# Branch gates of a transformer block through the hyperbolic tangent instead of the sigmoid

## The reference, cut to what matters

```
ya = einsum('bsw,wd->bsd', o_att, w_branch_att)
yh = einsum('bsw,wd->bsd', o_hg, w_branch_hg)
g = jax.nn.sigmoid(gate_logits.astype(f32)).reshape(B, S, N_BRANCHES, D)
merged = g[:, :, 0] * ya + g[:, :, 1] * yh
mixed = einsum('bsd,de->bse', merged, w_out)
x = x + gate1 * mixed
```

## Time and profile before

| | |
|---|---|
| median of 3 runs | 2164.25 us (2162.42 to 2166.67) |
| profiled execution, its own time | 2162.72 us |
| its span | 2160.9 us |
| TensorE matmul busy | 1957.4 us, 91% of the span |
| VectorE busy | 656.9 us, 30% |
| ScalarE busy | 450.5 us, 21% |
| mean granted TensorE clock | 0.964 |

### The profile page before, as it was taken

One profiled execution on the slowest core, in us unless ns is written; L12 is line 12 of the kernel. 1 busy time (PEld: TensorE's weight loads), 2 busy tenths in 40 slices (PEclk: granted clock), 3 DMA queues, 4 the chain that ended last, 5 costly groups with the idle time before them and its releaser, 6 DMA issues.

```text
span 2160.9 us, 20391 instructions
## 1 busy us (share of the span) xinstructions
PE 1957.4 (91%) x8746; PEld 1168.4 (54%) x8746; DVE 656.9 (30%) x915; ACT 450.5 (21%) x664; POOL 29.6 (1%) x41
## 2 busy tenths in 40 slices
PE   3989989899959999898989989898889999999998
PEld 2876766466833434343433434343334487888887
DVE  6474464472140020111002020111027713222333
ACT  4347455410010101010000101010020303222222
POOL 0000000000000000000000000000030000000000
PEclk9999999999979999999999999999989999999999
DMA  7211111475419999999999999999952013323210
GB/s 289 79 41 57 60 39 40 153 275 188 199 61 413 416 416 416 417 416 417 418 418 418 417 416 416 417 417 416 418 176 78 20 59 117 98 94 99 95 63 39
DMA packets 143791, 513.43 MB, mean 238 GB/s; under 512 B 7891, under 2 KB 70355, under 8 KB 107731
## 3 DMA queue, kind: packets, MB, share of 16 engines
q1 hardware_dynamic: 139328, 486.57, 57.3%
q10 hardware_dynamic: 4374, 25.56, 3.1%
HBM read 510.00 MB, written 2.10 MB: 237 GB/s over the span
## 4 chain that ended last, share of the span: by engine, by line
PE 69%; DMA 19%; DVE 5%; ACT 4%; issue 2%; SPq 1%; POOL 0%; ACTq 0%; DVEq 0%; POOLq 0%
PE ps L1015 12%; DMA work<-in_w_exp_up 10%; PE ps L492 6%; PE ps L979 6%; PE ps L515 5%; DMA ring<-in_w_exp_up 5%; PE ps L1158 5%; PE ps L1119 4%; PE ps L1118 4%; PE ps L1117 4%; PE ps L508 3%; PE ps L937 3%; PE ps L510 3%; PE ps L509 3%; PE ps L669 2%
## 5 line engine op out<-in xcount | busy, mean ns | idle before, releaser
L979 PE MATMUL ps<-work 128*64 128x512 f32 x1208 | 356.1, 594 | 28.4 <-DMA work<-in_w_exp_up 27.5
L979 PE MATMUL ps<-ring,work 128*64 128x512 f32 x720 | 219.4, 594 | 16.3 <-DMA ring<-in_w_exp_up 15.9
L979 PEld LDWEIGHTS ps<-work 128*64 128x64 f32 x1208 | 117.1, 137 | 204.2 <-issue 148.9
L1974 DVE TENSOR_TENSOR work<-work,ps 64x512 f32<-64x512 f32 x64 | 42.0, 691 | 486.9 <-ACT work L1490 486.3
L1490 ACT ACTIVATE work<-ps 64x512 f32<-64x512 f32 x64 | 32.6, 585 | 750.7 <-PE ps L979 750.7
L1015 PE MATMUL ps<-work 128*64 128x512 f32 x608 | 155.0, 661 | 4.7 <-issue 4.2
L492 PE MATMUL ps<-work,ring 128*128 128x512 f32 x320 | 139.1, 593 | 1.5 <-ACT work L1388 0.8
L1117 PE MATMUL ps<-xh,wh 128*128 128x512 f32 x352 | 137.0, 389 | 0.0
L1119 PE MATMUL ps<-xh,wl 128*128 128x512 f32 x352 | 136.9, 389 | 0.0
L1118 PE MATMUL ps<-xl,wh 128*128 128x512 f32 x352 | 136.9, 389 | 0.0
L979 PEld LDWEIGHTS ps<-ring,work 128*64 128x64 f32 x720 | 72.6, 137 | 119.0 <-issue 86.7
(11 more groups left out here) (253 smaller groups left out, 2444.4 us busy)
## 6 DMA issues: line engine op xcount, KB each, us to landing
work<-in_w_exp_gate SPq DMA_DIRECT2D x76, 1024.0 KB, 24.4
work<-in_w_exp_down SPq DMA_DIRECT2D x76, 1024.0 KB, 20.8
work<-in_w_exp_up SPq DMA_DIRECT2D x75, 1024.0 KB, 25.6
ring<-in_w_exp_gate SPq DMA_DIRECT2D x45, 1024.0 KB, 24.4
ring<-in_w_exp_up SPq DMA_DIRECT2D x45, 1024.0 KB, 25.5
ring<-in_w_exp_down SPq DMA_DIRECT2D x44, 1024.0 KB, 21.6
ring<-in_w_in SPq DMA_DIRECT2D x27, 1024.0 KB, 5.4
work<-in_ada_w ACTq DMA_DIRECT2D x16, 1024.0 KB, 5.1
```

The costliest lines, as they stand in the source:

```text
L979: i = e.matmul(PS[64 * gu:64 * gu + 64, fb, :], at(XET + 128 * k + 64 * z, 64), flat(key)[:, 512 * fb:512 * fb + 512], start=(k == 0), sto ...
```

## The change

All sixteen gate ACTIVATEs compute tanh of half the logit. The one that is missing is added by VectorE in the instruction that multiplies gate and branch product: a tensor_tensor becomes a scalar_tensor_tensor (in0 + 1.0) * in1. The factor one half is put on the copy of GATE1's row; GATE2's copy has the factor 1.0.

```
-                    e.activation(at(rooms(x), 512), bank(2), ACT.Sigmoid).then_inc(s["bg_a"], 1)
+                    e.activation(at(rooms(x), 512), bank(2), ACT.Tanh, scale=0.5).then_inc(s["bg_a"], 1)
...
-            def ada_row(n, dst):
+            def ada_row(n, dst, factor):
                 for i in range(2):
                     e.wait_ge(s["ar_pe"], n + i + 1)
-                    e.activation(at(dst + 512 * i, 512), bank(6 + i), ACT.Copy).then_inc(s["ar_a"], 1)
+                    e.activation(at(dst + 512 * i, 512), bank(6 + i), ACT.Copy, scale=factor).then_inc(s["ar_a"], 1)
...
-                e.activation(at(mt[4 * (d % 2)], 512), bank(4 * (d % 2)), ACT.Sigmoid).then_inc(s["mg_sa"], 1)
+                e.activation(at(mt[4 * (d % 2)], 512), bank(4 * (d % 2)), ACT.Tanh, scale=0.5).then_inc(s["mg_sa"], 1)
...
-                e.activation(at(mt[4 * (d % 2) + 1], 512), bank(4 * (d % 2) + 1), ACT.Sigmoid).then_inc(s["mg_sb"], 1)
+                e.activation(at(mt[4 * (d % 2) + 1], 512), bank(4 * (d % 2) + 1), ACT.Tanh, scale=0.5).then_inc(s["mg_sb"], 1)
...
-                    ada_row(0, GATE1)
+                    ada_row(0, GATE1, 0.5)
...
-            ada_row(2, GATE2)
+            ada_row(2, GATE2, 1.0)
...
-                e.tensor_tensor(at(s0, 512), at(s0, 512), bank(4 * (d % 2) + 2), ALU.mult).then_inc(s["mg_a"], 1)
+                e.scalar_tensor_tensor(out=at(s0, 512), in0=at(s0, 512), scalar=1.0, in1=bank(4 * (d % 2) + 2), op0=ALU.add, op1=ALU.mult).then_inc(s["mg_a"], 1)
...
-                e.tensor_tensor(at(s1, 512), at(s1, 512), bank(4 * (d % 2) + 3), ALU.mult).then_inc(s["mg_b"], 1)
+                e.scalar_tensor_tensor(out=at(s1, 512), in0=at(s1, 512), scalar=1.0, in1=bank(4 * (d % 2) + 3), op0=ALU.add, op1=ALU.mult).then_inc(s["mg_b"], 1)
```

## The result

The changed kernel runs in 2156.24 us (median of 5, 2154.68 to 2156.53) against 2164.25 before; the ratio is 0.9949 with an interval of 0.9938 to 0.9961. Two further comparisons gave 0.9949 (0.9928 to 0.9969) and 0.9950 (0.9938 to 0.9961). So it is 0.5% faster, about 11.0 us by the ratio, where 6.6 us were forecast. The two medians alone differ by 8.0 us, less than the ratio says, and 2156.24 lies inside the range; in the two further comparisons the medians differ by 11.5 and 12.3 us. The direction and the mechanism held, the size was too small.

What follows compares the result with a forecast made beforehand. TensorE bounds the kernel, so ScalarE's loads pay only where TensorE waits through them. Gains of 1.02 + 0.27 + 1.87 + 1.57 + 1.29 + 0.60 = 6.62 us, less 0.05, give 2157.7 us; range for 8 in 10: 2153.5 to 2163.

Steps and rivals of the forecast that it cites:

- The loads: ScalarE's table loads at the first eight gates, the attention's exponentials and the merge: 16 go, 20.5 us of ScalarE.
- the tables stay: Rival: Tanh has a load of its own and Exp is loaded back; about 2164.3 us, chance 0.10.
- The waits: TensorE's waits from 298.56 to 406.65 shorten by 1.02, 0.27, 1.87, 1.29 and 0.60 us without the loads.
- the two that were to stay: TensorE's waits of 2.67 us at 324.11 and 2.21 us at 373.65: nothing won at either.
- What is added: Tanh for Sigmoid taken as 0 us; VectorE's products with a scalar added taken as +0.05 us.
- The clock: TensorE's half clock behind the 3.03 us wait at 344.71 goes, worth 1.57 us.
- the fall at 324.11: Half clock behind TensorE's 2.67 us wait, L669 taking 3.65 us against 2.02: expected to stay, nothing won.
- this case for one place: The clock at 324.11 could hold by a small shift: 1.7 us more, a gain of 8.3 us.
- Slower by the clock: Rival: tables stay, waits grow and the clock falls at three more places; 5.2 us slower, 2169.4 us, chance 0.04.
- Given back behind the merge: Rival: TensorE waits for transfers behind the merge; gain only 0 to 4 us, 2160.3 to 2164.3, chance 0.07.

Runs made afterwards that it cites:

- before_again: The kernel before, without any edit, timed against itself: ratio 1.0009.
- merge_only_tanh: The changed kernel with the first eight gates sigmoids again (products times 2.0 for d < 4), tanh only in the merge: ratio 1.0004 to the kernel before.
- x0_sigmoid: The changed kernel with the gate x = 0 alone as a sigmoid, its product times 2.0: ratio 0.9981 to the kernel before.
- after_reorder: The changed kernel with the gate x = 2 and its rounding one step later on ScalarE and VectorE: ratio 0.9959 to the kernel before.
- reorder_dve: The changed kernel with the gate x = 2 one step later on ScalarE, VectorE's half subtraction two steps later: ratio 0.9935 to the kernel before.
- after_third: The changed kernel without any edit, compared a third time with the kernel before: ratio 0.9950.
- x3_sigmoid: The changed kernel with the gate x = 3 alone as a sigmoid, its product times 2.0: ratio 0.9981 to the kernel before.

## Why the prediction was right in kind and wrong in size

*The loads.* Right: 16 of 16 went, ScalarE's busy time fell from 450.5 to 429.9 us. The rival that the tables stay is out. What the trace of before couldn't show, a Tanh without a load behind Exp and in front of it, is there now, as the Trainium skill has it (ScalarE: Activation LUTs, "Table sets: the hidden batching unit"); its other rule, a logarithm and an exponential with one load, isn't what this program does in either trace.

*The waits.* Nearly right: 5.05 us forecast, 5.6 found (the stretch is 133.56 - 124.78 = 8.78 us shorter, and its two falls took 1.63 and 1.54). From mark to mark of TensorE: 1.1 for 1.02, 0.5 for 0.27, 2.0 for 1.87, 1.4 for 1.29, 0.6 for 0.60, and 0 for the two that were to stay. A load was priced 1.30 us, from its start to that of the next ACTIVATE. That was a little low: without a load the exponential starts before the rounding ahead of it has ended. Timelines of ScalarE, one line of the kernel before and two of the changed one:

```profile
293.62 1.05 ACT L1222 ACTIVATE fwh<-ring 128x1024 fp32r<-128x1024 f32 x1
```

```profile
294.00 1.05 ACT L1222 ACTIVATE fwh<-ring 128x1024 fp32r<-128x1024 f32 x1
...
294.94 0.68 ACT L1377 ACTIVATE work<-ps,stay 128x512 f32<-128x512 f32 x1
```

From the start of L1222 to that of the exponential it was 2.37 us and is 0.94, so a load on ScalarE's path is worth 1.43 us. No drain besides it showed.

*What is added.* Right: 0.60 us for Tanh; 0.68 to 0.69 for the product, so 0 where 0.05 was taken.

*The clock: the term that was mis-sized.* The forecast took back one fall, 1.57 us, and let the one behind the wait of 2.67 us "stay too". The price was right: traces show 1.54 us for the fall that was taken back. But the fall at 324.11, put at nothing, was worth 1.63, and the number of falls was taken as fixed: the first trace of before has two falls, two further traces of kernels with all eight sigmoids and their order unchanged have three, and none stands in the four traces of kernels with the first eight gates tanh and their order unchanged. So the clock had 3.2 us to give in the first trace and up to 1.6 more in the others, not 1.57. Together with the waits the stretch is 8.8 us shorter than in the first trace of before and 10.4 shorter than in before_again. The measured 11.0 us has an interval of about 2.5 to each side. The failing step was the inference from the lengths of the waits: that 2.67 us brings the clock down and 2.46, 2.21 and 2.12 don't. The same wait of 2.67 us came with a fall in four traces (before, before_again, merge_only_tanh, x0_sigmoid) and without one in six; 2.12 with a fall in two and without in two; 2.21 in after_reorder and reorder_dve with, in eleven without. The length is not nothing: 3.03 to 3.05 us had a fall in five of five, 2.46 in none of five. What decides besides the length seems to be where the wait lies in relation to what came before: x0_sigmoid left this wait its length and moved it by 1.1 us, and the fall came back. That rests on one trace of x0_sigmoid, and no run here shows how the chip chooses. The forecast had named this case for one place (8.3 us, with the clock at 324.11 holding; the traces have 8.8) and then gave it too little room; the case that the clock holds everywhere in the stretch should have been priced and the range have reached to 2152. That the result fell just outside the range and not just inside is chance: 0.3 us is far below what the runs can tell.

*Slower by the clock.* The rival was thought to need longer waits. after_reorder shows that a kernel with shorter waits can gain a fall: of 1.7 us won up to that fall, from the first wait on, the fall took 0.9 back.

*Given back behind the merge.* Half open. The profiled executions of before and after differ by 6.5 us only, because the part from the output projection on took 1635.44 in the one and 1637.76 in the other; but the changed kernel has 1635.16 in after_third, so that is no effect of the change. Between merge and output projection a wait for the branch weights of 2.2 to 2.6 us stands in three traces (before_again, x3_sigmoid, x0_sigmoid), with a fall beside it, and they take 117 us there where the others take 112.5 to 115. The same wait is 0.68 us in the first trace of before, 0.51 in that of the changed kernel and 1.80 in that of after_reorder. That would account for the ratios of x3_sigmoid and x0_sigmoid, and perhaps for a part of the 11.0 us. One trace for each kernel doesn't tell how often it comes, so it isn't shown.

## What to carry to other kernels

Price a table load only where the timeline has it between the engine's last input and the instruction that ends another engine's wait: of the 15 loads that went from this stretch about six moved the end at all, worth 5.6 of their 19.2 us. Then ask what the next engine in line allows; VectorE set the floor of two waits. And take the clock's falls in one trace as one draw: with waits of 2 to 3 us in a row, price every one of them with and without a fall, since a shift of 1 us far ahead of a wait may bring or take it.

## What the runs showed of the hardware that was not expected

The granted clock can fall to half behind a TensorE wait of 2.12 us (before_again) and hold behind one of 2.67 us (all four traces with the first eight gates tanh in their old order). The timing ahead seems to matter: with a wait 25 us earlier made 1.16 us longer, the clock fell behind an unchanged wait of 2.67 us, in the one trace of x0_sigmoid. Two traces of one program had two and three falls in the same stretch. A fall costs 1.3 to 1.6 us here with TensorE at work throughout, and 0.9 where a wait behind it took up part. A table load takes 1.28 us and moves the exponential behind it by 1.43: without it the exponential starts 0.11 us before the rounding ahead of it ends.
